# Splitting the first weights on VectorE and moving GpSimd, ScalarE and TensorE work around five waits in a two-block model kernel

## The reference, cut to what matters

```python
mod = jnp.dot(silu(c), ada_w[l]) + ada_b[l]                 # "ada": shifts, scales, gates
h = modulate(rms_norm(x, norm1_g[l]), sh1, sc1)
z = jnp.einsum('bsd,de->bse', h, w_in[l]) + b_in[l]         # z_qk, z_gate, z_n
qk = silu(causal_dwconv(concat([mq, mk]), conv_w, conv_b))  # four taps; then mLSTM
qa, ka = rope(aq), rope(ak)                                 # angles by sin and cos
...                                                         # two mixers, merged, w_out
x = x + g1 * (merged @ w_out)
h = modulate(rms_norm(x, norm2_g[l]), sh2, sc2)             # "norm 1" of the kernel
x = x + g2 * ((silu(h @ w_gate) * (h @ w_up)) @ w_down)     # ff_g, ff_u, down
x = rms_norm(x, normf_g)                                    # "norm 3"
# second block, layer 0: hn = rmsnorm(x, mix_norm)           -> "norm 4", then e_pv, e_u, ...
#   memory attention: k, v = mem_n @ wkv                     -> x_k0, x_v0
#   peer_ffn: every token gathers 128 rows of 16384 experts  -> rows_a, rows_b, rows_c
```

## Time and profile before

| | us |
|---|---|
| median of 3 runs | 2375.37 |
| lowest, highest | 2373.08, 2378.62 |
| the profiled execution | 2373.18 |
| its span (first to last instruction) | 2371.4 |

### The profile page before, as it was taken

How to read it: one execution, slowest core, us unless ns; L and a number is a source line. 1 busy time by engine, 2 the same in 40 slices (tenths; PEclk the granted TensorE clock), 3 DMA queues, 4 the chain that set the end, 5 groups by cost and what they waited for, 6 DMA issues and landing times.

```text
span 2371.4 us, 25342 instructions
## 1 busy us (share of the span) xinstructions
PE 2080.1 (88%) x8542; PEld 1303.9 (55%) x8542; DVE 1477.2 (62%) x3713; ACT 783.5 (33%) x1787; POOL 982.3 (41%) x693
## 2 busy tenths in 40 slices
PE   7999999999999899998778987878999979777876
PEld 3865759987866655543235645544565546233322
DVE  6655242126231578887677767768786667877755
ACT  2332234344322233333334343233434232333332
POOL 2630547888721233433433333233323233344542
PEclk9999999999999999999999998999999989898999
DMA  8446444545442799999999999999999999999997
GB/s 328 167 161 211 167 158 164 187 173 191 174 149 78 272 422 424 419 390 414 425 421 423 411 405 420 420 417 384 421 395 381 377 420 370 402 415 424 410 425 295
DMA packets 139762, 777.37 MB, mean 328 GB/s; under 512 B 15512, under 2 KB 17688, under 8 KB 73072
## 3 DMA queue, kind: packets, MB, share of 16 engines
q0 software_dynamic: 75792, 547.25, 56.0%
q1 hardware_dynamic: 63696, 228.44, 26.2%
q10 hardware_dynamic: 144, 0.05, 0.0%
HBM read 774.62 MB, written 1.06 MB: 327 GB/s over the span
## 4 chain that ended last, share of the span: by engine, by line
PE 50%; DMA 23%; DVE 19%; ACT 4%; issue 2%; POOL 1%; DVEq 0%; SPq 0%; ACTq 0%; POOLq 0%
PE banks L815 16%; PE banks L908 15%; DMA rows_c<-in_uv,p_eid 9%; PE banks L945 7%; DMA rows_b<-in_uv,p_eid 7%; DMA W<-in_weights 5%; PE banks L1128 2%; DVE rows_b L2374 2%; PE banks L982 2%; DVE arena L1949 2%; DVE rows_c L2374 2%; DMA arena<-in_uv,p_eid 2%; DVE arena L2374 2%; PE banks L1356 1%; ACT arena L1552 1%
## 5 line engine op out<-in xcount | busy, mean ns | idle before, releaser
L710 POOL TENSOR_TENSOR W_lo<-W,W_hi 128x1024 fp32r<-128x1024 f32 x160 | 392.9, 2465 | 185.3 <-ACT W_hi L1499 184.2
L908 PE MATMUL banks<-arena 128*128 128x512 f32 x712 | 352.1, 632 | 86.9 <-ACT arena L1561 86.6
L762 POOL DMA_INDIRECT arena<-in_uv,p_eid x192 | 221.9, 1156 | 498.0 <-PE banks L908 392.8
L908 PE MATMUL banks<-rows_b,arena 128*128 128x512 f32 x668 | 325.1, 626 | 58.0 <-ACT arena L1561 58.0
L762 POOL DMA_INDIRECT rows_b<-in_uv,p_eid x192 | 210.6, 1097 | 301.2 <-PE banks L908 234.3
L1550 ACT ACTIVATE arena<-arena 128x2 f32<-128x2 f32 x256 | 52.0, 203 | 826.8 <-DVE arena L1955 825.4
L2374 DVE SCALAR_TENSOR_TENSOR arena<-arena,H 128x1024 f32<-128x1024 f32 x192 | 232.8, 1224 | 100.9 <-DMA arena<-in_uv,p_eid 97.9
L2374 DVE SCALAR_TENSOR_TENSOR rows_b<-rows_b,H 128x1024 f32<-128x1024 f32 x192 | 232.2, 1224 | 100.1 <-DMA rows_b<-in_uv,p_eid 98.3
L908 PEld LDWEIGHTS banks<-arena 128*128 128x128 f32 x712 | 135.2, 200 | 264.0 <-issue 143.2
L1499 ACT ACTIVATE W_hi<-W 128x1024 fp32r<-128x1024 f32 x160 | 168.2, 1058 | 311.5 <-PE banks L815 218.8
L908 PE MATMUL banks<-rows_c,arena 128*128 128x512 f32 x460 | 224.0, 630 | 47.4 <-ACT arena L1561 47.3
(11 more groups left out here) (304 smaller groups left out, 3141.3 us busy)
## 6 DMA issues: line engine op xcount, KB each, us to landing
W<-in_weights SPq DMA_DIRECT2D x408, 512.0 KB
gain<-in_rows SPq DMA_DIRECT2D x7, 512.0 KB, 12.1
gain<-in_rows POOLq DMA_DIRECT2D x6, 512.0 KB, 5.3
arena<-in_keys SPq DMA_DIRECT2D x3, 1024.0 KB, 8.6
arena<-in_uv,p_eid POOLq DMA_INDIRECT x192
rows_b<-in_uv,p_eid POOLq DMA_INDIRECT x192
arena<-in_rows POOLq DMA_DIRECT2D x1, 2048.0 KB, 13.3
rows_c<-in_uv,p_eid POOLq DMA_INDIRECT x128
```

Source lines behind the costliest of these rows:

```text
L710: po.tensor_tensor(W_lo[:, slot, :], W[:, (PARTS * n + part) % RAW_RING, :], W_hi[:, slot, :].bitcast(F32), ALU.subtract).then_inc(S_("lo_ ...
L762: po.indirect_dma_start(rows[slot], None, io[f"uv{l}"], bass.IndirectOffsetOnAxis(ap=p_eid[:, t, j:j + 1], axis=0))\
L908: mm = pe.matmul(banks[:, plan.bank(f"p_v{c}", b), :], diag[:, m % DIAGS, :], rows[slot][:, D + b * BLK:D + (b + 1) * BLK], start=j == 0, ...
```

## The change

- Bank order: ada_r0 takes the first bank, bias_rows the second.
- TensorE: waits for `const_in` first, makes three dummy matmuls, then `ada_row(0)`; `bias_rows` with its two waits comes after that. Five dummy matmuls instead of eight ahead of z_qk.
- VectorE: `sum_ada(0)` ahead of the copy of `bias_rows`; the lows of parts 0, 1 and 2 of z_qk are made here (`first_low`), between the modulated tiles and their splits.
- GpSimd: starts its lows at part 3, and waits for three `lo_made` before; waits for `h_ready` of norm 1 (both halves) ahead of the lows of ff_u0.
- ScalarE: `high` of three z_qk parts ahead of `HT_hi` instead of two; of parts 20 to 22 of the split order ahead of the waits for `conv_ready` and `angle_ready`; of three x_v0 parts instead of one ahead of norm 4.

```diff
@@ make_plan
+    p.add("ada_r0", taker="scalar")
     p.add("bias_rows")
-    p.add("ada_r0", taker="scalar")
@@ gpsimd
-            lows = [0]
+            lows = [SPLIT_RING]
+            po.wait_ge(S_("lo_made"), SPLIT_RING)
...
-                    for part in range(PARTS):
+                    for part in range(skipped, PARTS):
...
             low("w_out", 1)
+            po.wait_ge(S_("h_ready"), 2 * NT)
             low("ff_u0")
@@ tensor
-            pe.wait_ge(S_("rel_in"), 16)
-            pe.wait_ge(S_("onehot_in"), 16)
-            pe.matmul(claim("bias_rows")[0:8, :], rel_sb[:], onehot, start=True, stop=True).then_inc(pe_filled, 1)
             pe.wait_ge(S_("const_in"), 16)
+            busy("ada_r0", 3)
...
             ada_row(0)
+            pe.wait_ge(S_("rel_in"), 16)
+            pe.wait_ge(S_("onehot_in"), 16)
+            pe.matmul(claim("bias_rows")[0:8, :], rel_sb[:], onehot, start=True, stop=True).then_inc(pe_filled, 1)
...
-            busy("z_qk", 8)
+            busy("z_qk", 5)
@@ scalar
-            high("z_qk", 0, 2)
+            high("z_qk", 0, 3)
...
-            high("z_qk", 2)
+            high("z_qk", 3)
             high("z_qk", i=1)
             high("z_n")
             high("z_n", i=1)
             high("z_n", i=2)
+            high("z_n", 0, 3, i=3)
             act.wait_ge(S_("conv_ready"), 1)
...
-            high("z_n", i=3)
+            high("z_n", 3, i=3)
...
-            high("x_v0", 0, 1)
+            high("x_v0", 0, 3)
             norm(4, X, lambda t: act.wait_ge(S_("h_ready"), 3 * NT + t + 1))
-            high("x_v0", 1)
+            high("x_v0", 3)
@@ vector
-            v.wait_ge(S_("onehot_in"), 16)
+            v.wait_ge(S_("silu_c"), 1)
+            sum_ada(0)
             bank = filled(v, "bias_rows")
             step.free(v.tensor_copy(rb_sb, bank[0:8, :]), "bias_rows")
-            v.wait_ge(S_("silu_c"), 1)
-            sum_ada(0)
             sum_ada(1)
...
+            def first_low(part):
+                v.wait_ge(S_("hi_made"), part + 1)
+                step(v.tensor_tensor(W_lo[:, part, :], W[:, (PARTS * tile_no["z_qk"] + part) % RAW_RING, :],
+                                     W_hi[:, part, :].bitcast(F32), ALU.subtract), "lo_made")
             modulated(0)
             modulated(1)
+            first_low(0)
             split_h0(0)
             split_h0(1)
+            first_low(1)
             modulated(2)
             modulated(3)
             split_h0(2)
             split_h0(3)
+            first_low(2)
```

More of the change, by code:

```diff
@@ L703, in low @@
                 for n in range(first + (i or 0), first + (i or 0) + count):
-                    assert parts_before(n) == lows[0]
-                    for part in range(PARTS):
+                    skipped = SPLIT_RING if n == tile_no["z_qk"] else 0
+                    assert parts_before(n) + skipped == lows[0]
+                    for part in range(skipped, PARTS):
                         slot = lows[0] % SPLIT_RING
```

## The result

The changed kernel takes 2361.51 us in the median of six runs (2353.35 to 2364.68), against 2374.55 (2372.59 to 2378.62) for six runs of the kernel before beside it. The ratio is 0.9937, with a 95% interval of 0.9922 to 0.9951: faster by 13.0 us, where 17.6 were forecast. Two later series of the same kernel gave 0.9947 (0.993 to 0.9964) and 0.9949 (0.993 to 0.9968), so about 12 to 15 us in all. Its profiled execution has a span of 2351.5 us and is the fastest of its runs.

What follows compares the result with a forecast made beforehand. Up to about 830 us a chain of TensorE's split products, with short pieces of other engines between, bounds the kernel; gains 8.3 + 3.9 + 3.4 + 2.0 = 17.6 us, from median 2375.37, forecast 2357.8 us, range 2351.5 to 2366.

Steps and rivals of the forecast that it cites:

- the rival in which the gather stage swallows it: Gather stage: its DMA would start by a clock of its own, leaving under 4.7 us only in part; 2375, chance 0.04.
- the one in which it collects more half clock: Gather stage: more TensorE pauses followed by half clock eat the gain or make the kernel slower; 2380, chance 0.03.
- Term 1: Start of TensorE: waiting for constants, then dummy passes, delays `ada_row(0)`; a loss of 1.5 us.
- the order is dear because SyncE may load part 6 and on only when TensorE has used part 0 and on: Start: a later `ada_row(0)` delays SyncE's load on which `sum_ada(1)` starts, moving all that follows by 1.5 us.
- Term 2: z_qk: lows 0 to 2 on VectorE avoid the lock, part 2 starts earlier, a half clock goes; a gain of 9.8 us.
- Term 3: z_n: earlier highs move TensorE's pause to part 23 and shrink it to 1.6 us; a gain of 3.9 us.
- The rival in which the pause only moves: z_n: the pause moves without shrinking, so that gain is 0; sum 13.7, time 2361.7, chance 0.2.
- Term 4: Norm 1: GpSimd rests until `H` is whole, so two stretched VectorE steps go; a gain of 3.4 us.
- TensorE, after T1 and its dummies, is due at 354.1: Norm 1: with `H` whole at 351.2, TensorE is due for ff_u0 at 354.1 instead of 357.46.
- Term 5: Norms 3 and 4: earlier x_v0 highs move TensorE's pause to part 3, shrunk to 2.6 us; a gain of 2.0 us.
- T4 waiting for `H` or for the banks of x_k0 longer than 2 us: Norm 4, at T4: a wait longer than 2 us here was named as a sign that the prediction is wrong.
- the rival said 3.5: Norm 4 starves behind the lows: a loss of 3.5 us there; sum 12.1, time 2363.3, chance 0.17.

Runs made afterwards that it cites:

- after: First profiled execution of the changed kernel, the fastest of its runs: span 2351.5 us; median of its six runs 2361.51 us.
- again_b: The changed kernel unchanged, third profiled execution, run on the same chip as `combined`: median 2362.59 us, ratio 0.9949.
- again: The changed kernel run once more unchanged, second profiled execution: median 2362.85 us, ratio 0.9947.
- undo_lows: Changed kernel with z_qk lows 0 to 2 back on GpSimd, order of TensorE and ScalarE as changed: 2367.44 us, ratio 0.9977.
- undo_norm1: Changed kernel without GpSimd's wait for both halves of norm 1 ahead of the ff_u0 lows: 2366.39 us, ratio 0.9976.
- combined: Changed kernel with angles and Sin moved early, two x_v0 parts ahead of norm 4, ten dummies instead of twelve ahead of T1: 2354.14 us, ratio 0.9926.
- x_v0_two: Changed kernel with only two x_v0 parts ahead of norm 4 instead of three: 2357.7 us, ratio 0.9941.
- no_dummy: Changed kernel without the three dummy products ahead of `ada_row(0)`: 2360.63 us, ratio 0.9952.

## Why the prediction was right, and where it was short

The sign and the range were right (2357.8 forecast, 2361.51 measured), and so was the frame: from the first gather to the end every execution takes 1568 to 1574 us (before: 1571.8). What is won ahead of it arrives at the end within that spread, and neither the rival in which the gather stage swallows it nor the one in which it collects more half clock happened.

The sum was 17.6 us; the mean of three executions has 12.1 at the first gather. By stretches, forecast against measured:

| stretch | term | forecast | measured |
|---|---|---|---|
| start to the copy | 1 | -1.5 | -0.9 |
| the copy to z_gate | 2 | 9.8 | 9.5 |
| z_gate to rotation | 3 | 3.9 | 3.4 |
| rotation to merge T | none | 0 | -1.7 |
| merge T to ff_u0 | 4 | 3.4 | 2.5 |
| T2 to T4 | 5 | 2.0 | -0.5 |
| the rest | none | 0 | -0.3 |

(Rounded; measured is the mean of three executions against one of the kernel before.)

**Term 1.** The size fits: 0.9 us lost, with 1.5 forecast and 0.8 as its lower bound. `ada_row(0)` starts at 13.5 (12.9 forecast; its terms, 7.6 and 5.1, give 12.7) and ends at 20.5 (20.4). Whether it was lost in the way forecast is open. The step "the order is dear because SyncE may load part 6 and on only when TensorE has used part 0 and on" got no support: with `ada_row(0)` 4.2 us earlier the load was issued 1.8 us earlier and landed within 0.05 us of the same time. But over all ten executions with the dummies the copy is 1.1 us later than before, in a spread of 2.8, so what moved it isn't settled.

**Term 2.** Right in size and picture. VectorE's lows take 1.24 (1.22 forecast), no VectorE subtraction is over 2 us before 50, the half clock of 58.4 is gone, part 2 starts at 50.59 (49.7, plus the 1.5 of term 1), z_gate at 68.20 (68.5). What the sum does not tell is where it comes from: 5.3 of the 9.5 us are VectorE's lows, and these work mostly by making low 0 before GpSimd's six DMAs are out. The prediction has that start of part 0 in its sum without naming what held it before. The other 4.2 come with the new order even where the splits stand behind the lock for 9.04 us.

**Term 3.** 3.4 against 3.9 at the rotation's start, 3.0 at the transposes behind it, by another way than the one worked out. The pause moved ahead of part 23, as said, but TensorE is idle there for 2.0 to 2.8 us instead of 1.6. The convolution starts 9.8 us earlier now, with z_gate, and meets more lows than I counted (twelve steps over 1.5 us in `after`, nine before), and ends only 3.3 earlier (`conv_ready` at 110.3). The angles behind it, which I had let crawl beside three lows, ran between lows in 2.7 us in `after` and `again_b`; in `again` one step of them took 2.24. By the rule of the page "SBUF — State Buffer" of the Trainium skill (section "Who interferes with whom") the prediction had estimated a pause of 2.6, and that is nearer to the measured 2.0 to 2.8 than my 1.6, though the lows blocked the convolution rather than the angles. The rival in which the pause only moves would have kept the old 57.0; it fell, as the stretch is at most 55.1, but `again` has its half clock and keeps only 1.9 of the 3.9.

**Term 4.** The mechanism was right, as undoing it brings both stretched steps back. The size was 2.5 and not 3.4 (the two stretches by themselves give 1.2 and 2.1, so 3.3): "TensorE, after T1 and its dummies, is due at 354.1" left the dummies themselves out as the next bound. They end at 339.01, when `H` is all but whole, and T1 can't start before; with two dummies fewer the stretch lost another 0.8.

**Term 5.** This step failed, and it is the largest part of the shortfall. The pause did move to part 3, with 2.2 us idle for 2.6. But the forecast of 2.0 took an average of how a step fares beside the lows, and the stretch has two outcomes, 158.6 (2.4 better) and 163.0 (2.0 worse), and went to the worse in five of eight executions. The prediction had asked for a sign of being wrong, "T4 waiting for `H` or for the banks of x_k0 longer than 2 us", and it was seen in those five (3.7 us idle), with a loss of 2.0 where the rival said 3.5: five of the twelve steps of `rstd` take over 2 us, not all, but then the first long tile of `H` loses too, and TensorE gets half a clock. The better outcome came twice by half a clock at part 3, which opened a gap between the lows, and once by a tile of `H` that went first; the prediction had neither. The rival's chance of 0.17 was too low for what was in hand: the prediction named bounds from 4 to -3.5 and then counted on the middle of them.

**Outside the terms.** From the rotation to merge T the table gives 181.1 us before, 181.8 and 181.9 in `again_b` and `after`, and 184.8 in `again`, with its 10.3 us at half clock. No edit lies there, and I had assumed no change. The 0.7 us of the first two is the rotation's first instruction again: from `a_T` to merge T they take 168.2 us, as before, and `again` alone takes 171.9. The other changed kernels take 181.2 to 182.2 from the rotation. Whether the earlier start makes such a spell likelier stays open.

## What to carry to other kernels

Where two engines share a lock, look for the long instructions on both sides that start within a few tenths of a microsecond of each other, and move one of them: a gain that hangs on which of them goes first was nothing on the average here. Where a stretch has two outcomes, go back to the first row that differs; here it was a granted clock, some 10 us ahead of the tile that seemed to decide. When a part is undone, read which wait ends last before giving its price a name: the lock came back in `undo_lows`, and TensorE waited for something else. Read a gain of 2 us over several executions of the same kernel, by stretches between fixed points, because one profile can show the best of them. When a wait is removed, look at what was put in as a filler for it (dummy passes here), since the filler is the next wait.

## What the runs showed of the hardware

- Two instructions that block each other, 0.29 us apart: the one that starts first by the records does not always go first. VectorE's 128x1024 tile took 1.28 us in `after` and 3.79 in `again` with the low 0.29 us behind it in both. In the six executions in which GpSimd issues the gain's DMA right ahead of that low (0.57 us, over the start of VectorE's instruction), VectorE lost in five. In the four in which the low comes out of a wait for its `high` instead (0.18, 0.21, 0.46 and 0.54 us behind VectorE's start, in `undo_norm1`, `combined`, `undo_lows` and `x_v0_two`), VectorE went first in all. That the DMA's issue is the cause is not shown; no kernel moved it alone. The page "SBUF — State Buffer" of the Trainium skill (section "Who interferes with whom") says that issue order decides who blocks. The four agree, and the five of six don't, if the records' starts are the order of issue.
- Lows back to back hold VectorE where lows with a gap between them let it through. In norm 4 of `after` four lows without a gap (9.47 us) go with four `rstd` steps of 2.3 us; in `undo_norm1` GpSimd stands still for 0.82 us after three, and the next three steps take 0.16 us each.
- Whether half a clock follows a pause of TensorE is not told by the pause's length in these traces. Ahead of part 23 of z_n TensorE is idle for 2.84 us in `again_b` and for 2.85 in `no_dummy`: behind the one the granted clock is 1.00, behind the other 0.50 for 3.4 us. Behind 1.95 us (`again`, to 118.27) it is 0.50 too.
- A VectorE instruction that reads a bank and one SBUF tile is not held by the lows. The `HT_lo` splits out of banks behind norm 1 take 0.68 to 0.69 us each in `after` (340.21 to 342.70), with lows running beside them from 339.24 on; a split of the same size out of two SBUF tiles took 8.31 us beside three lows in `undo_lows`.
